# Modulation sections moved into the attentions, and a router with its first selection by token tile

## What is computed

```python
mod = (silu_c @ w_mod[l] + b_mod[l])[:, None, :]
sh_a, sc_a, gt_a, sh_f, sc_f, gt_f = jnp.split(mod, 6, axis=-1)
h = modln(x, g_attn[l], sh_a, sc_a)        # rmsnorm(x) * (1 + scale) + shift
y, yc = token_mixers(h, hc, w_in[l], ...)  # conv, two attentions, gated merge, w_o
x = x + gt_a * y
h2 = modln(x, g_ffn[l], sh_f, sc_f)
yt = hier_moe(...)                         # top-1 of 4 groups, top-2 of its 8 experts
x = x + gt_f * yt
```

## Time and profile before

| | |
|---|---|
| median of three runs | 1362.85 us (1360.55, 1362.85, 1365.0) |
| the profiled execution, its own time | 1366.03 us |
| its span in the trace | 1364.2 us |
| busy: PE, PEld, DVE, ACT, POOL | 90%, 69%, 48%, 32%, 13% |
| the chain that ended last: PE, DVE, issue, DMA, ACT | 80%, 8%, 4%, 4%, 2% |

### The profile page before, as it was taken

One profiled execution on the slowest core, in us unless ns is written; L12 is line 12 of the kernel. 1 busy time (PEld: TensorE's weight loads), 2 busy tenths in 40 slices (PEclk: granted clock), 3 DMA queues, 4 the chain that ended last, 5 costly groups with the idle time before them and its releaser, 6 DMA issues.

```text
span 1364.2 us, 22180 instructions
## 1 busy us (share of the span) xinstructions
PE 1226.1 (90%) x8966; PEld 936.5 (69%) x8966; DVE 649.0 (48%) x1503; ACT 438.0 (32%) x1041; POOL 171.6 (13%) x212
## 2 busy tenths in 40 slices
PE   4999888899998989899999789998998868889986
PEld 2788754688887966666666469965998755555652
DVE  1544586464345463422221285667776545233334
ACT  3533366433334350010000364356665510000001
POOL 1810000111011300100000401001111200000001
PEclk9899899999999999999999889999998879999998
DMA  9994145423323279999999985248555859999995
GB/s 353 314 351 151 62 142 192 131 93 93 93 93 124 93 276 417 360 411 414 416 386 373 385 206 155 93 154 264 180 183 188 322 214 419 419 415 415 388 373 185
DMA packets 131831, 351.14 MB, mean 257 GB/s; under 512 B 23054, under 2 KB 84726, under 8 KB 108561
## 3 DMA queue, kind: packets, MB, share of 16 engines
q1 hardware_dynamic: 118144, 317.69, 63.1%
q0 software_dynamic: 12304, 30.37, 6.6%
q10 hardware_dynamic: 1280, 1.66, 0.4%
HBM read 330.53 MB, written 28.86 MB: 263 GB/s over the span
## 4 chain that ended last, share of the span: by engine, by line
PE 80%; DVE 8%; issue 4%; DMA 4%; ACT 2%; POOL 0%; SPq 0%; DVEq 0%; ACTq 0%; POOLq 0%
PE banks L1021 33%; PE banks L1263 16%; PE banks L1277 8%; PE banks L1255 6%; PE banks L1189 4%; PE banks L958 3%; PE banks L1117 2%; PE banks L1132 2%; PE banks L1102 2%; DMA expert_rows<-arena,rows_u 1%; DMA ring<-in_w_in 1%; DMA ring<-in_w_mod 1%; DMA ring<-in_w_e_up 1%; DVE arena L2352 1%; DVE att L2080 1%
## 5 line engine op out<-in xcount | busy, mean ns | idle before, releaser
L1994 DVE TENSOR_TENSOR w_lo_r<-ring,w_hi_r 128x256 fp32r<-128x256 f32 x480 | 222.7, 474 | 241.2 <-ACT w_hi_r L1618 240.1
L1618 ACT ACTIVATE w_hi_r<-ring 128x256 fp32r<-128x256 f32 x480 | 197.4, 416 | 304.6 <-PE banks L1021 254.9
L1263 PE MATMUL banks<-ring,arena 128*64 128x256 f32 x2016 | 233.8, 385 | 28.1 <-issue 11.5
L1021 PE MATMUL banks<-h_hi_r,w_hi_r 128*128 128x512 f32 (+1 forms) x640 | 221.8, 347 | 6.1 <-DVE h_lo_r L1938 4.7
L1263 PEld LDWEIGHTS banks<-ring,arena 128*64 128x64 f32 x2016 | 162.5, 138 | 89.0 <-issue 37.4
L1021 PE MATMUL banks<-h_lo_r,w_hi_r 128*128 128x512 f32 (+1 forms) x640 | 220.2, 344 | 0.0
L1021 PE MATMUL banks<-h_hi_r,w_lo_r 128*128 128x512 f32 (+1 forms) x640 | 220.1, 344 | 0.0
L1021 PEld LDWEIGHTS banks<-h_hi_r,w_hi_r 128*128 128x128 f32 x640 | 122.9, 192 | 22.5 <-ACT arena L1588 4.8
L1021 PEld LDWEIGHTS banks<-h_lo_r,w_hi_r 128*128 128x128 f32 x640 | 123.0, 192 | 13.8
L1021 PEld LDWEIGHTS banks<-h_hi_r,w_lo_r 128*128 128x128 f32 x640 | 122.8, 192 | 13.8
L1277 PE MATMUL banks<-ring,att 128*64 128x512 f32 x424 | 119.3, 604 | 14.1 <-DVE att L2369 7.4
(11 more groups left out here) (269 smaller groups left out, 1726.3 us busy)
## 6 DMA issues: line engine op xcount, KB each, us to landing
ring<-in_w_e_gate SPq DMA_DIRECT2D x64, 1024.0 KB, 8.7
ring<-in_w_e_up SPq DMA_DIRECT2D x62, 1024.0 KB, 9.3
ring<-in_w_e_down SPq DMA_DIRECT2D x53, 1024.0 KB, 9.3
ring<-in_w_mod SPq DMA_DIRECT2D x48, 1024.0 KB, 6.6
ring<-in_w_in SPq DMA_DIRECT2D x38, 1024.0 KB, 5.5
expert_rows<-att POOLq DMA_DIRECT2D x23, 512.0 KB, 20.3
ring<-in_w_o SPq DMA_DIRECT2D x8, 1024.0 KB, 5.1
ring<-in_w_branch SPq DMA_DIRECT2D x8, 640.0 KB, 4.5
```

The lines of the kernel that those rows point to most:

```text
L1021: ins = mm(out_ap, a, b, start=k == 0 and p_ == 0, stop=k == KD - 1 and p_ == 2)
L1263: ins = mm(banks[e * CAP:(e + 1) * CAP, bank, 0:DE], x[:, k, e * CAP:(e + 1) * CAP], w[:, k * DE:(k + 1) * DE], start=k == 0, stop=k == KD ...
L1618: fn(w_hi[:, u % AHEAD, :, :], chunk(key)[:, q * KU:(q + 1) * KU, :], ACT.Copy).then_inc(w_hi_ready, 1)
L1994: v.tensor_tensor(w_lo[:, u % AHEAD, :, :], chunk(key)[:, q * KU:(q + 1) * KU, :], w_hi[:, u % AHEAD, :, :].bitcast(F32), ALU.subtract).th ...
```

## The change

Four things are rewritten. (1) `MOD_ROUTE` goes; its sections join the attentions: six sections, 24 chunks, in attention 0 in the order 4, 3, 2, 5 of layer 0 and 1, 0 of layer 1; four sections, 16 chunks, in attention 1. `MOD_STEP` gives each chunk its step. In layer 0, steps 0 to 7 have one each, steps 10 and 17 two, the other steps from 11 to 23 one, and sections end at steps 3, 7, 12, 16, 19 and 23. In layer 1, steps 0, 1, 3, 6 and 9 have two, steps 2, 4, 7, 8, 10 and 11 one, and sections end at steps 1, 4, 8 and 11. All sections use one bank, and so do the columns, which are made at step 8 of layer 0 and step 5 of layer 1. (2) In layer 0 three row tiles are turned back ahead of the ranks instead of two, and one after. (3) The first selection of a layer is written and used by token tile, and the first operand tiles are taken by DVE (even ones) and ACT (odd ones, `take_first`). (4) ACT does the router's exponentials after its row tiles, and DVE's sum over the first of them moves from `place` to `weights`. The stream of weights is reordered to match. Cut to its core:

```diff
@@ -111,9 +111,8 @@
-MOD_IN = [[(0, 2), (0, 4), (0, 3)], [(1, 2), (1, 4), (1, 3)]]
-MOD_ROUTE = [[(0, 5), (1, 1), (1, 0)], [(1, 5)]]
-MODS = [(0, 1), (0, 0)] + MOD_IN[0] + MOD_ROUTE[0] + MOD_IN[1] + MOD_ROUTE[1]
+MOD_IN = [[(0, 4), (0, 3), (0, 2), (0, 5), (1, 1), (1, 0)], [(1, 4), (1, 3), (1, 2), (1, 5)]]
+MODS = [(0, 1), (0, 0)] + MOD_IN[0] + MOD_IN[1]
@@ -137,7 +136,6 @@
         out += [("wo", l, c) for c in range(4)]
-        out += [("mod", k, 4 * sec + j) for k, sec in MOD_ROUTE[l] for j in range(4)]
@@ -558,17 +558,14 @@
         MOD_BANK, O_BANK = 7, 6
-        ROW_BANKS = [(3, 0), (4, 5), (3, 0), (4, 5)]
-        ROUTE_BANK = {(0, 5): 0, (1, 1): 7, (1, 0): 6, (1, 5): 0}
-
-        def mod_bank(l, sec):
-
-            return ROUTE_BANK.get((l, sec), MOD_BANK)
+        ROW_BANKS = [(3, 0), (4, 5), (6, 7), (3, 0)]
+        F_COL = {4: 256, 3: 256 + 2 * KD}
+        F_COL_STEP = [8, 5]
+        MOD_STEP = [[0, 1, 2, 3, 4, 5, 6, 7] + [10 + 14 * q // 16 for q in range(16)], [5 * q // 8 for q in range(8)] + [6 + 6 * q // 8 for q in range(8)]]
...
-            n = 4 * len(MOD_IN[l])
-            return range(n * s // len(STEPS[l]), n * (s + 1) // len(STEPS[l]))
+            return [q for q, at in enumerate(MOD_STEP[l]) if at == s]
@@ -949,13 +946,16 @@
                     pe.wait_ge(cond_ready, 2)
-                if n and j2 == 0 and (l, sec) not in ROUTE_BANK:
+                if n and j2 == 0:
                     pe.wait_ge(mod_out, n)
+                for m in range(DEPTH):
+                    if j2 == 0 and (l, sec) == MOD_IN[m][2]:
+                        pe.wait_ge(f_col_ready, 2 * (m + 1))
...
-                        ins = mm(banks[32 * q:32 * q + 32, mod_bank(l, sec), 0:CW], cond32[:, 2 * j2 + k, :],
+                        ins = mm(banks[32 * q:32 * q + 32, MOD_BANK, 0:CW], cond32[:, 2 * j2 + k, :],
@@ -975,13 +975,14 @@
             def ffn_columns(l):
-                for sec, bank in ((4, 6), (3, 7)):
-                    pe.wait_ge(mod_out, MOD_AT[(l, sec)] + 1)
+                for sec in (4, 3):
+                    pe.wait_ge(mod_out, MOD_AT[MOD_IN[l][1]] + 1)
                     for k in range(KD):
+                        at = F_COL[sec] + 2 * k
                         for j in range(4):
-                            ins = mm(banks[32 * j:32 * j + 32, bank, 2 * k:2 * k + 2], modr[:, l, sec, k::KD],
+                            ins = mm(banks[32 * j:32 * j + 32, MOD_BANK, at:at + 2], modr[:, l, sec, k::KD],
                                      ident[:, 32 * j:32 * j + 2], start=True, stop=True)
-                    ins.then_inc(f_cols_done, 1)
+                ins.then_inc(f_cols_done, 1)
@@ -1151,6 +1152,10 @@
                             mod(*MOD_IN[l][i // 4], i % 4)
+                        if s - 1 == F_COL_STEP[l]:
+                            ffn_columns(l)
+                pe.wait_ge(f_col_ready, 2 * (l + 1))
+                pe.wait_ge(mod_out, 2 + len(MOD_IN[0]) + l * len(MOD_IN[1]))
@@ -1225,8 +1230,8 @@
                 for tt in tiles:
-                    if tt >= 2:
-                        pe.wait_ge(th_hi_ready, tt - 1)
+                    if tt == 3:
+                        pe.wait_ge(th_hi_ready, 1)
@@ -1309,17 +1314,13 @@
                 nt = QT[l]
-                pe.wait_ge(sel_ready, n + 1)
                 if l == 0:
-                    pe.wait_ge(th_hi_ready, 3)
+                    pe.wait_ge(th_hi_ready, 4)
                 picked = sel[n % 2]
-                for k in range(KD):
-                    for key in MOD_ROUTE[l][1:]:
-                        if k == ROUTE_BANK[key]:
-                            pe.wait_ge(mod_out, MOD_AT[key] + 1)
-                    for tt in range(nt):
-                        if k == 0:
-                            pe.wait_ge(th_hi_ready, QT0[l] + tt + 1)
+                for tt in range(nt):
+                    pe.wait_ge(th_hi_ready, QT0[l] + tt + 1)
+                    pe.wait_ge(sel_first, QT0[l] + tt + 1)
+                    for k in range(KD):
@@ -1335,6 +1336,8 @@
                     pe.wait_ge(xeT_ready, lin(i, 4 * (n // 2 + 1), 2 * PPI))
+                    if p == 0:
+                        pe.wait_ge(xeT_act, l + 1)
@@ -1494,25 +1497,14 @@
                 out_proj(l)
-                pe.wait_ge(upd_ready, 4 * QT0[l] + 3 * QT[l])
-                for j2 in range(4):
-                    mod(*MOD_ROUTE[l][0], j2)
                 pe.wait_ge(upd_ready, 4 * (QT0[l] + QT[l]))
-                ffn_columns(l)
-                pe.wait_ge(mod_out, MOD_AT[MOD_ROUTE[l][0]] + 1)
...
-                    turn_rows((0, 1))
-                for k, sec in MOD_ROUTE[l][1:2]:
-                    for j2 in range(4):
-                        mod(k, sec, j2)
+                    turn_rows((0, 1, 2))
...
-                    turn_rows((2, 3))
-                for k, sec in MOD_ROUTE[l][2:]:
-                    for j2 in range(4):
-                        mod(k, sec, j2)
+                    turn_rows((3,))
@@ -1719,19 +1711,19 @@
                 fn(lgT[0][:, 0:QN[l]], banks[0:NR, 0, 0:QN[l]], ACT.Copy).then_inc(lgT_out, 1)
+                if l == 0:
+                    for tt in range(4):
+                        act.wait_ge(h_rows, tt + 1)
+                        for dst in (htok[:, tt, :], th_hi[:, tt, :]):
+                            for half, b in enumerate(ROW_BANKS[tt]):
+                                ins = fn(dst[:, half * 512:half * 512 + 512], banks[:, b, :], ACT.Copy)
+                        ins.then_inc(th_hi_ready, 1)
                 for r, (dst, src) in enumerate((
-                    (prod[:, 0, 0:nt, 0:8], prod[:, 0, 0:nt, 0:8]),
+                    (g8[:, 0:nt, :], g8[:, 0:nt, :]),
...
-                    if l == 0:
-                        for tt in (2 * r, 2 * r + 1):
-                            act.wait_ge(h_rows, tt + 1)
-                            for dst in (htok[:, tt, :], th_hi[:, tt, :]):
-                                for half, b in enumerate(ROW_BANKS[tt]):
-                                    ins = fn(dst[:, half * 512:half * 512 + 512], banks[:, b, :], ACT.Copy)
-                            ins.then_inc(th_hi_ready, 1)
@@ -1764,7 +1756,20 @@
                 fn(own_t[:, 0:QN[l]], banks[:, X_BANK, 0:QN[l]], ACT.Copy).then_inc(own_t_ready, 1)
+            def take_first(l):
+
+                n = Q0[l]
+                for q in range(4):
+                    k = 2 * q + 1
+                    act.wait_ge(xe_turned, 4 * n + q + 1)
+                    if l:
+                        ins = fn(xeT[n % 2][:, k, :], banks[:, k, 0:SEQ], ACT.Identity, bias=f_add[:, k, 0:1], scale=f_mul[:, k, 0:1])
+                    else:
+                        ins = fn(xeT[n % 2][:, k, :], banks[:, k, 0:SEQ], ACT.Copy)
+                ins.then_inc(xeT_act, 1)
+
             def experts(l):
+                take_first(l)
@@ -1958,14 +1963,8 @@
                 v.reciprocal(stat[:, 12:16], stat[:, 8:12]).then_inc(f_rstd_ready, 1)
-                mod_add(*MOD_ROUTE[l][0])
...
-                    if tt == nt // 2:
-                        for n, (dst, bank) in enumerate(((f_mul, 6), (f_add, 7))):
-                            dve.wait_ge(f_cols_done, 2 * l + n + 1)
-                            v.tensor_copy(dst[:, :, :], banks[:, bank, 0:2 * KD].rearrange("p (k s) -> p k s", s=2))\
-                                .then_inc(f_col_ready, 1)
@@ -2071,6 +2070,12 @@
                                 mod_add(*MOD_IN[l][i // 4])
+                        if s - 2 == F_COL_STEP[l]:
+                            dve.wait_ge(f_cols_done, l + 1)
+                            for sec, dst in ((4, f_mul), (3, f_add)):
+                                at = F_COL[sec]
+                                v.tensor_copy(dst[:, :, :], banks[:, MOD_BANK, at:at + 2 * KD].rearrange("p (k s) -> p k s", s=2))\
+                                    .then_inc(f_col_ready, 1)
@@ -2170,10 +2175,10 @@
                 for tt in range(nt):
-                    v.max_index(idx_g[:, tt, :], top_g[:, tt, :], g8[:, tt, :])
-                v.tensor_tensor(prod[:, 0, 0:nt, 0:8], g8[:, 0:nt, :], top_g[:, 0:nt, 0:1].to_broadcast([P, nt, 8]),
+                    ins = v.max_index(idx_g[:, tt, :], top_g[:, tt, :], g8[:, tt, :])
+                link(ins)
+                v.tensor_tensor(g8[:, 0:nt, :], g8[:, 0:nt, :], top_g[:, 0:nt, 0:1].to_broadcast([P, nt, 8]),
                                 ALU.subtract).then_inc(router_exp_in, 1)
-                dve.wait_ge(router_exp_in, 2 * l + 1)
@@ -2206,6 +2211,7 @@
                 dve.wait_ge(router_exp, 2 * l + 2)
+                link(v.tensor_reduce(rt[:, 4:4 + nt], g8[:, 0:nt, :], AX.X, ALU.add))
@@ -2244,7 +2250,13 @@
                 if d == 0:
-                    ins = v.tensor_copy(slots, slots_f[:, :, 0:QT[l]])
+                    v.tensor_copy(slots, slots_f[:, :, 0:QT[l]]).then_inc(sel_slot_ready, 1)
+                    dve.wait_ge(sel_slot_ready, n + 1)
+                    for tt in range(QT[l]):
```

(16 more changed lines are left out.)

10 lines of the change are left out of this document (6 added, 4 removed).

## The result

The changed kernel takes 1379.8 us (median of 1375.2, 1378.5, 1381.0 and 1381.3), the kernel before in the same comparison 1361.7; the ratio, which is one of means, is **1.0123 (1.0091 to 1.0155)**, so by it the kernel is slower by 16.7 us (the medians are 18.1 us apart). The forecast was slower, but by 5, and 1379.8 lies beyond its 1377.

The account below looks back on a forecast made before the run. TensorE bounds the kernel through a chain of handovers and waits; attentions +9.4 and +9.2, clock +1.5, routers -6.1 and -8.9 gave +5.1 us, so a median of 1368.0 us, range 1355 to 1377.

Parts of the forecast that it names:

- the chain: Whole kernel: the chain of waits ending last runs almost wholly over TensorE, with attentions a loop of handovers; no size.
- the places: Attentions: DVE waits 2 us for TensorE's chunk or columns at steps 8, 12, 16 (layer 0) and 4, 5, 8 (layer 1).
- the sign: Whole kernel: the change makes it slower, by +5.1 us; chance of slower 0.55.
- 2.4 late and 2.0 net: Attentions, section ending on an even step: odd turning 2.4 us late, some 0.4 made good, 2.0 each.
- the gates' clock: Expert gate matmuls behind the routers: less idle time ahead lets them run faster, -1.3 us behind router 0, -1.2 behind router 1.
- the term on the clock in the attentions: Both attentions: new waits drop TensorE's clock for one value product in each layer, +1.5 us (0 to 5).
- The rival on the clock: Attentions: low clock slows value products, scores and turnings, four pairs by 2 us each, +8; 1376 us, chance 0.15.
- router 0, -6.1 us: Layer 0's router up to and with the gates: turning -1.0, ranks -2.1, rank copy to first gate -1.7, gates -1.3.
- The first step: Router 0, turning of h: begins 3.3 us sooner but takes some 2.3 longer at the lower clock, leaving -1.0.
- the step from the ranks' copy to the first gate: Router 0: selection by tile and shared operand tiles cut 15.2 us to 13.5, -1.7 us (between -3.1 and +0.2).
- half of them 1.7 us longer: Router 0, first 32 selection matmuls: 4.0 us, with half of them 1.7 us longer at the lower clock.
- The rule of the Trainium skill: Router 0, turning of h: gaps throw TensorE to the lower clock; without the rule -3.3 us, by it -1.0.

Follow-up runs that it names:

- e11: The kernel before, unchanged, traced once more to see scatter; its router 1 took 35.2 us instead of 37.9.
- e3: The changed kernel with DVE's section additions and its copies of f_mul and f_add moved behind the scaling of the next step; ratio 1.0049.
- e6: The changed kernel with those late additions, column matmuls in two halves at successive steps, layer 1's third section a step later; ratio 1.0028.

## Why the prediction was wrong

*Right: the chain, the places, the sign.* DVE's waits came where they were put, at steps 8, 12 and 16 of layer 0 and 4, 5 and 8 of layer 1 (2.7 to 4.1 us, where 2 was forecast), and PE stood 1.7 to 2.2 us for the odd turning at all of them but step 5; the forecast had 2.4 late and 2.0 net. Steps 0 to 7 of layer 0 cost 0.8 us between value products (forecast 0.2), steps 16 and 17 together 2.4 (2.6). Router 1 fell by 7.9 us against the earlier trace rows with -7.7 forecast without the gates' clock: its turning ended 5.3 us sooner (forecast 5.0), the selection began another 0.5 sooner (0.8), and from there to the gates it was 2.1 shorter (1.9, for the operand tiles). Some of this hit is luck of the trace: against e11, where the kernel before stopped only 2.91 us in the turning, router 1 fell by 5.2. The gates of router 1 did get their clock back (7.13 us instead of 8.54, in the second pair of 8.81; forecast -1.2).

*Wrong: the term on the clock in the attentions, 1.5 us.* This is the step that failed. Between the value products at 197.41 and 228.16 of layer 0, over steps 8 to 12, the changed kernel lost 9.2 us where waits and chunks had been priced at 6 and the clock at 0.75. In layer 1 it lost 7.8 from the value product at 927.96 to that at 952.51, where 3.7 had been priced, and the clock at 0.75. The granted clock was 0.57 from 204 to 216 us:

```profile
204.00:216.00 12.00, 8.75 (x56) 0.57 0.00 1
```

The prediction took one value product at half speed in each layer. It was two turnings and a value product in layer 0 (1.97, 1.90 and 3.68 us for 1.09, 1.09 and 1.95), and a turning, the scores and a value product in layer 1 (1.97, 2.08 and 3.49 for 1.09, 1.13 and 1.95), each late for the next handover: 6.8 us longer together. The rival on the clock named this and put it at +8; it had 0.15. It had it begin once PE's waits pass some 2.5 us, and that was not so: the clock fell behind waits of 2.00 and 2.20 us next to the columns, and at other steps not behind 1.67, 1.82 and 2.20. e3 and e6 took both away, the waits ahead of the scaling and most of the low clock, and 24.8 us of loss in the attentions became 7; how much of the 17.8 is the waits and how much the clock behind them, no run parts.

*Wrong: router 0, -6.1 us, of which 0.9 came.* 1.3 of the 6.1 were for the gates, which stand behind this window, so it is 0.9 of 4.8. The first step held: the turning began 3.1 us sooner and took 2.0 more (forecast 3.3 and 2.3). The ranks' copy came 2.5 us sooner (3.1). What failed is the step from the ranks' copy to the first gate, put at 13.5 us against the 15.2 of before: it took 16.9. The last row tile was ready at +5.5 (forecast +3.6 to +5.4), the first 32 matmuls took 6.4 to the next group (5.7 with "half of them 1.7 us longer"), the last 32 took 4.0 (3.9), and the gates came 1.0 later (0.5). The 13.5 goes only with the early end of the row tile; with the late end the prediction's own numbers give 15.5. The late end came because ranks and row tile ran at half speed too (1.33 and 1.89 us instead of 0.75 and 1.06 for the ranks' later groups, 1.95 instead of 1.07 for the tile), and for these the prediction had no term: it charged the clock for the turning of h and for half of the 32 matmuls, while some 20 us of the router ran at the lower level (0.76 over 41.9 us is the upper one for 52% of it). The gates did run at full clock, 7.13 us instead of 8.8. But the kernel before had 7.13 too in its second trace, so that this gain was chance of the one trace. The table load of the exponentials was hidden, as said: it stood at 519.7 us, ACT's first operand tile at 529.4.

*The sum.* With the means of both pairs, forecast and measured: attentions +20.1 and +24.8, router 0 without gates -4.8 and -0.9, router 1 without gates -7.7 and -6.5, gates -2.5 and -2.4. The differences, 4.7 + 3.9 + 1.2 + 0.1, make 9.9 us; the timed difference is 11.6 above the forecast, and the rest is within what single traces scatter. The first two misses are mostly the clock, left out in the same way: priced at one or two instruction groups, where it lay on every one of a chain of handovers. The third is no more than the kernel before differs from itself (37.9 and 35.2 us). The rule of the Trainium skill that the prediction had weighed for the turning alone (TensorE: Matmul & The Clock Gate, section HAM oscillation) tells of a loop in which each burst behind a gap pays for the lower clock anew. The traces agree in router 0, with 5.79 against 3.81 us for the turning of h and 6.57 against 4.02 for the selection; in the attentions a turning behind a wait of 2.20 us took 1.97 us at one step and 1.09 at another.
